# A filter network inside the preceding output projection, and a layer norm by token halves, in a four-layer encoder

## The reference

```python
for i in range(DEPTH):                       # 4 layers
    mod = silu(c) @ mod_w[i] + mod_b[i]
    shift, scale, gate = split(mod, 3)
    hn = rmsnorm(x, norm_g[i]) * (1 + scale) + shift
    # mixer i % 3: 0 = RWKV-7, 1 = Hyena, 2 = Conformer convolution
    x = x + gate * mixer(hn)                 # each mixer ends in (...) @ w_out
# Hyena filters: z from positions, three times z = sin(freq * (z @ W + b)), then (z @ f_w_out) * window, normalised, rfft
# Conformer:
a, b, g = split(h @ w_in, 3)
u = depthwise_conv(a * sigmoid(b), dw_w, dw_b)      # 31 taps
u = silu(layernorm(u, ln_g, ln_b))
return (u * silu(g)) @ w_out
```

## Time and profile before

| | |
|---|---|
| median of 3 runs | 4082.78 us (4078.05 to 4083.08) |
| the profiled execution | 4076.46 us, its span 4074.7 us |
| PE busy | 3435.6 us, 84% of the span |
| DVE busy | 2096.6 us, 51% |
| ACT busy | 1126.1 us, 28% |
| mean granted TensorE clock | 0.925 of full |

### The profile page before, as it was taken

One profiled execution on the slowest core, in us unless ns is written; L12 is line 12 of the kernel. 1 busy time (PEld: TensorE's weight loads), 2 busy tenths in 40 slices (PEclk: granted clock), 3 DMA queues, 4 the chain that ended last, 5 costly groups with the idle time before them and its releaser, 6 DMA issues. The chain is left out here.

```text
span 4074.7 us, 97171 instructions
## 1 busy us (share of the span) xinstructions
PE 3435.6 (84%) x41792; PEld 2461.1 (60%) x41792; DVE 2096.6 (51%) x4027; ACT 1126.1 (28%) x2792; POOL 0.2 (0%) x4
## 2 busy tenths in 40 slices
PE   4978888888888777989987899487788998889978
PEld 3556766766776644666664555254477667676665
DVE  2254544544454325776773299723455545555542
ACT  2023333332333222333231111112133333333330
POOL 0000000000000000000000000000000000000000
PEclk9988999999999888999998899688899999999989
DMA  3021101111111130010101111021000000000003
GB/s 142 31 80 50 66 26 46 60 33 45 55 50 40 62 108 29 30 43 32 33 36 52 64 52 52 16 89 41 27 14 19 19 12 14 14 19 18 13 20 106
DMA packets 65826, 179.05 MB, mean 44 GB/s; under 512 B 9105, under 2 KB 22545, under 8 KB 65425
## 3 DMA queue, kind: packets, MB, share of 16 engines
q1 hardware_dynamic: 53472, 144.02, 10.5%
q10 hardware_dynamic: 11952, 29.04, 1.9%
HBM read 157.30 MB, written 15.73 MB: 42 GB/s over the span
## 5 line engine op out<-in xcount | busy, mean ns | idle before, releaser
L1632 DVE SCALAR_TENSOR_TENSOR RBF<-bank,ID 128x256 bf16<-128x256 f32 x480 | 192.8, 421 | 409.6 <-PE bank L615 400.7
L954 PE MATMUL bank<-BY,W 128*128 128x384 f32 x1024 | 345.9, 498 | 48.0 <-DVEq L1709 35.2
L813 PE MATMUL bank<-BH,W 128*128 128x384 f32 x1024 | 342.8, 490 | 6.9 <-ACT HZ L1218 6.6
L954 PEld LDWEIGHTS bank<-BY,W 128*128 128x128 f32 x1024 | 196.7, 194 | 181.8 <-DVEq L1709 35.9
L813 PEld LDWEIGHTS bank<-BH,W 128*128 128x128 f32 x1024 | 191.8, 192 | 137.0 <-issue 16.7
L954 PE MATMUL bank<-BX,W 128*128 128x384 f32 x640 | 220.4, 500 | 61.4 <-DVE BX L1955 61.0
L1040 PE MATMUL bank<-BH,W 128*128 128x384 f32 x768 | 250.7, 490 | 15.8 <-DMA W<-in_cf_w_in 15.8
L1678 DVE SCALAR_TENSOR_TENSOR CACC<-CU,CV,CACC 128x798 f32<-128x798 f32 x232 | 224.1, 1041 | 0.0
L735 PE MATMUL bank<-BH,W 128*128 128x384 f32 x512 | 214.3, 549 | 8.9 <-DVE BH L1955 8.9
L1040 PEld LDWEIGHTS bank<-BH,W 128*128 128x128 f32 x768 | 147.2, 192 | 119.8 <-DMA W<-in_cf_w_in 16.9
L954 PEld LDWEIGHTS bank<-BX,W 128*128 128x128 f32 x640 | 121.3, 194 | 160.5 <-issue 67.6
(11 more groups left out here) (273 smaller groups left out, 6378.5 us busy)
## 6 DMA issues: line engine op xcount, KB each, us to landing
W<-in_mod_w SPq DMA_DIRECT2D x96, 512.0 KB, 3.6
W<-in_rw_w_in SPq DMA_DIRECT2D x68, 512.0 KB, 3.9
W<-in_hy_w_in SPq DMA_DIRECT2D x32, 512.0 KB, 6.8
x_scratch<-BX ACTq DMA_DIRECT2D x32, 384.0 KB, 4.2
W<-in_cf_w_in SPq DMA_DIRECT2D x24, 512.0 KB, 3.5
W<-in_rw_w_out SPq DMA_DIRECT2D x16, 512.0 KB, 4.2
W<-in_hy_w_out SPq DMA_DIRECT2D x8, 512.0 KB, 3.8
W<-in_cf_w_out SPq DMA_DIRECT2D x8, 512.0 KB, 4.2
```

Of the source, the lines that this page charges most:

```text
L813: mm = pe.matmul(pj(h), W[:, s, k, :], BH[:, k, tok(h)], start=(k == 0), stop=(k == KT - 1))
L954: mm = pe.matmul(pj(h), lhs(k), rhs(k, h), start=(k == 0), stop=(k == nk - 1))
L1632: v.scalar_tensor_tensor(RBF[:, d, :, :], xout(d), -1.0, bc(ID2[:, 1 if r < NBF else 0, :], GC), ALU.mult, ALU.add).then_inc(ir_ready, 1)
```

## The change

- The filter network of the Hyena layer runs inside the output projection of layer 0: its three matmul steps (`pe_mlp`) after products 0, 3 and 5, DVE's part in two pieces after each of tiles 1 to 6 (`dve_mlp`), ACT's sines after tiles 2, 4 and 6. It writes banks 4 and 5 in place of 2 and 3. DVE clears HU after tile 0. Its constants are loaded by SP between the first and second four weight tiles of that projection; the other Hyena constants, the first filter weights and the four weight tiles are issued behind the projection's, with no wait for BH. The two-tile buffer for x in layers 0 and 3 moves from TW to a part of HX.
- The vectors and first weight tiles of the Conformer are issued once the Hyena layer's outputs are complete, with no wait for BH.
- The layer norm of the Conformer: the mean is accumulated tile by tile inside the product loop (`means`, two tiles behind, banks 6 and 7). After it each step runs by token halves; the subtraction in four pieces. The squares are the loaded operand and one column of MEAN the moving one, so that the variance comes out token by token (3 columns per half); root and reciprocal are taken there, spread on a diagonal and multiplied out by PE, as in the RMS norm. Scale and root are applied in one instruction, and bias goes into the join and into ACT's tanh; the factor 0.25 goes into the gate vector.

```diff
-        XOUT = (TW, HZ, CACC)
+        XOUT = (HX[:, :, 0, :], HZ, CACC)
...
+        def before_hyena(l):
+            return l % 3 == 0 and l + 1 in layers
...
-        HY_CONST = ((ID, "idm"), (FWD, "hfwd"), (INV, "hinv"), (HZ[:, 0, :], "hz"), (HWF, "hwf"), (HB, "hb"), (HTW, "htw"), (HVA, "hyv"))
+        HY_MLP = ((HZ[:, 0, :], "hz"), (HWF, "hwf"), (HB, "hb"))
+        HY_CONST = ((ID, "idm"), (FWD, "hfwd"), (INV, "hinv"), (HTW, "htw"), (HVA, "hyv"))
...
-                    if first and s == 0:
-                        sp.wait_ge(h_ready, 2 * KT * (NRM[l] + 1))
-                        for dst, src in HY_CONST:
-                            sp.dma_start(dst[:], a[src]).then_inc(hyc_ready, 16)
-                        filt(j)
...
+            for dst, src in HY_CONST:
+                sp.dma_start(dst[:], a[src]).then_inc(hyc_ready, 16)
+            filt(0)
             one(0, True)
...
                 for s in range(slots):
                     load(s, source(0, s), free[s])
+                if between:
+                    between()
...
-                    sp.wait_ge(h_ready, 2 * KT * (NRM[l] + 1))
+                    sp.wait_ge(y_ready, NRM[l] * KT)
                     sp.dma_start(CVA[:, :, :], a["cfv"]).then_inc(cfv_ready, 16)
                     cf(0, True)
...
+                def mlp_constants():
+                    sp.wait_ge(y_ready, (NRM[l] + 1) * KT)
+                    for dst, src in HY_MLP:
+                        sp.dma_start(dst[:], a[src]).then_inc(hym_ready, 16)
+                tiles((l, "out"), 2, lambda i, s: cols(wout, i * 4 + s), None, mlp_constants if before_hyena(l) else None)
...
+        def pe_mlp(pe, i):
+            if i:
+                pe.wait_ge(mlp_sin, i)
+            else:
+                pe.wait_ge(hym_ready, 16 * len(HY_MLP))
+            for b, (n0, nt, ln) in enumerate(NTL):
+                mm = pe.matmul(NB[b][:, 0:ln], HWF[:, i, :], HZ[:, i % 2, n0 * P:n0 * P + ln], start=True, stop=True)
+            mm.then_inc(mlp_full, 1)
...
+                    if not chain:
+                        pe.wait_ge(mlp_sin, 3)
+                        pe.wait_ge(xn_ready, 2 * KT * (NRM[l] + 1))
...
-            for i in range(3):
-                if i:
-                    pe.wait_ge(mlp_sin, i)
-                else:
-                    pe.wait_ge(mlp_arg, 1)
-                for b, (n0, nt, ln) in enumerate(NTL):
-                    mm = pe.matmul(SC[b][:, 0:ln], HWF[:, i, :], HZ[:, i % 2, n0 * P:n0 * P + ln], start=True, stop=True)
-                mm.then_inc(mlp_full, 1)
-            pe.wait_ge(mlp_sin, 3)
...
+                    def means(k):
+                        pe.wait_ge(cf_conv, k + 1)
+                        for h in range(2):
+                            mm = pe.matmul((SQB, YB)[h][:, 0:HALF], MEAN, BD[:, k, tok(h)], start=(k == 0), stop=(k == KT - 1))
+                            if k == KT - 1:
+                                mm.then_inc(ln_mean, 1)
...
                                 mm.then_inc(cb_full[s][h], 1)
-                    base = plan[(l, "ln")][1]
-                    pe.wait_ge(cf_conv, KT)
-                    product(base, lambda k: MEAN, lambda k, h: BD[:, k, tok(h)], KT).then_inc(pj_full[1], 1)
+                            if s == 0 and j >= 2:
+                                means(j - 2)
+                    means(KT - 2)
+                    means(KT - 1)
                     for h in range(2):
-                        pe.wait_ge(pj_free[h], base + 2)
-                    for k in range(KT):
-                        pe.wait_ge(ln_sq, k + 1)
-                        for h in range(2):
-                            mm = pe.matmul(pj(h), MEAN, SQ[:, k % 2, tok(h)], start=(k == 0), stop=(k == KT - 1))
-                        mm.then_inc(ln_r, 1)
-                    pe.wait_ge(ln_r, KT)
-                    pe.sem_inc(pj_full[0], 1)
-                    pe.sem_inc(pj_full[1], 1)
+                        for k in range(KT):
+                            pe.wait_ge(ln_sq, h * KT + k + 1)
+                            for c in range(3):
+                                t = h * HALF + c * P
+                                mm = pe.matmul(SC[h][:, c:c + 1], SQ[:, k % 2, t:t + P], MEAN[:, 0:1], start=(k == 0 and c == 0),
+                                               stop=(k == KT - 1 and c == 2))
+                            mm.then_inc(ln_r, 1)
+                    for h in range(2):
+                        pe.wait_ge(ln_dg, h + 1)
+                        pe.matmul((SQB, YB)[h][:, 0:HALF], MEAN, SQ[:, 0, tok(h)], start=True, stop=True).then_inc(ln_full, 1)
...
+                        if before_hyena(l) and i * 4 + s in (0, 3, 5):
+                            pe_mlp(pe, (0, 3, 5).index(i * 4 + s))
...
-            act.activation(RN[:, 0, 0:1], EPSV[:, 0:1], ACT.Sqrt)
+            if not before_hyena(l):
+                act.activation(RN[:, 0, 0:1], EPSV[:, 0:1], ACT.Sqrt)
...
+                if before_hyena(l) and j in (2, 4, 6):
+                    i = j // 2 - 1
+                    act.wait_ge(mlp_arg, i + 1)
+                    act.activation(HZ[:, (i + 1) % 2, :], HZ[:, (i + 1) % 2, :], ACT.Sin).then_inc(mlp_sin, 1)
+                    if i == 2:
+                        act.activation(RN[:, 0, 0:1], EPSV[:, 0:1], ACT.Sqrt)
...
-                    act.wait_ge(ln_c, 1)
-                    for k in range(KT):
-                        if k >= 2:
-                            act.wait_ge(ln_r, k - 1)
-                        act.activation(SQ[:, k % 2, :], BD[:, k, :], ACT.Square).then_inc(ln_sq, 1)
+                    act.activation(RN[:, 0, 0:1], EPSV[:, 2:3], ACT.Sqrt)
                     for h in range(2):
-                        act.wait_ge(pj_full[h], base + 2)
-                        act.activation(RS[:, tok(h)], pj(h), ACT.Sqrt, bias=EPSV[:, 2:3]).then_inc(pj_free[h], 1)
-                    for k in range(KT):
-                        act.wait_ge(ln_t, k + 1)
-                        act.activation(TT[:, k % 2, :], BD[:, k, :], ACT.Tanh, scale=0.5).then_inc(cf_tanh, 1)
+                        for k in range(KT):
+                            act.wait_ge(ln_c, h * 2 + k // 4 + 1)
+                            if k >= 2:
+                                act.wait_ge(ln_r, h * KT + k - 1)
+                            act.activation(SQ[:, k % 2, tok(h)], BD[:, k, tok(h)], ACT.Square).then_inc(ln_sq, 1)
+                        act.wait_ge(ln_r, (h + 1) * KT)
+                        act.activation(RN[:, h, :], SC[h][:, 0:3], ACT.Sqrt, bias=EPSV[:, 2:3]).then_inc(ln_rt, 1)
+                    for h in range(2):
+                        for k in range(KT):
+                            act.wait_ge(ln_t, h * KT + k + 1)
+                            if k >= 2:
+                                act.wait_ge(ln_j, h * KT + k - 1)
+                            act.activation(CACC[:, k % 2, tok(h)], BD[:, k, tok(h)], ACT.Tanh, scale=0.5, bias=CLB[:, k:k + 1]).then_inc(cf_tanh, 1)
...
+        def dve_mlp(v, C, i, part):
+            two_pi_hi = 6.28125
+            two_pi_lo = float(2 * np.pi - two_pi_hi)
+            magic = 12582912.0
+            z, r = HZ[:, (i + 1) % 2, :], RS[:, :]
+            if part == 0:
+                v.wait_ge(mlp_full, i + 1)
+                for b, (n0, nt, ln) in enumerate(NTL):
+                    t = C.mark(v.tensor_scalar(z[:, n0 * P:n0 * P + ln], NB[b][:, 0:ln], HB[:, i:i + 1], HB[:, 3 + i:4 + i], ALU.add, ALU.mult))
+                C.wait(t)
+                C.link(v.tensor_scalar(r, z, float(1 / (2 * np.pi)), magic, ALU.mult, ALU.add))
+                C.link(v.tensor_scalar(r, r, magic, None, ALU.subtract))
+            else:
+                C.link(v.scalar_tensor_tensor(z, r, -two_pi_hi, z, ALU.mult, ALU.add))
+                C.link(v.scalar_tensor_tensor(z, r, -two_pi_lo, z, ALU.mult, ALU.add))
+                C.link(v.tensor_scalar(z, z, 3.1415925, -3.1415925, ALU.min, ALU.max))
+                v.sem_inc(mlp_arg, 1)
...
+                if before_hyena(l):
+                    if j == 0:
+                        C.link(v.memset(HU[:, :, :], 0.0))
+                    elif j < 7:
+                        dve_mlp(v, C, (j - 1) // 2, (j - 1) % 2)
...
+            mb = (SQB, YB)
+            gate = MOD[:, l * 24 + 16:l * 24 + 24, :]
+            C.mark(v.tensor_scalar(CLB[:, :], CVA[:, :, CONV + 2:CONV + 3].squeeze(2), 0.5, None, ALU.mult))
+            C.link(v.tensor_scalar(gate, gate, 0.25, None, ALU.mult))
+            def joined(k, h):
+                v.wait_ge(cf_tanh, KT * 2 + h * KT + k + 1)
+                v.scalar_tensor_tensor(BY[:, k, tok(h)], CACC[:, k % 2, tok(h)], 1.0, BY[:, k, tok(h)], ALU.add, ALU.mult).then_inc(ln_j, 1)
+                if h:
+                    v.wait_ge(ln_j, KT + k + 1)
+                    v.sem_inc(y_ready, 1)
+            v.wait_ge(ln_mean, 2)
             for h in range(2):
-                v.wait_ge(pj_full[h], base + 1)
```

(62 more changed lines are left out.)

6 lines of the change are left out of this document (2 added, 4 removed).

## The result

The changed kernel takes 4040.5 us (median; 4037.3 to 4047.5), the kernel before in the same comparison 4082.9: ratio 0.9897, 95% interval 0.9878 to 0.9917. It is faster, by 42 us. The forecast was 4012, 71 us faster, and the time lies outside the range. The profiled execution took 4037.31, its span is 4035.5.

A forecast was written before the change was run, and what follows sets the result against it. PE, busy 84% of the span, was taken to bound the kernel; gains of 45.0 + 15.8 + 10.1 = 70.9 us off the 4082.78 median gave 4012, range 3995 to 4029.

The forecast's parts named there:

- The sum at the three places: Forecast gains at the start of the Hyena layer, start of the Conformer layer and layer norm: 45.0 + 15.8 + 10.1 us.
- rival B: Layer norm gives nothing: its final loop stalls between VectorE and ScalarE, 2.3 us per half tile, not 1.7; 4022, chance 0.12.
- the forecast's own bounds: Likeliest case with all three gains at their upper or lower bounds: 45.0 + 17.0 + 14.5 (4006), 40.3 + 13 + 5 (4024).
- Hyena start: First Hyena products start with BH, gaining 49.0 us; the filter network costs 4.0 in the output projection: 45.0 net.
- rival C: Output projection: filter network isn't hidden, layers two and three wait in PE's queue for their sine; 4025, chance 0.07.
- Conformer start: Weights fetched before the norm, so PE starts at the first BH, 2294.65 in place of 2310.49: gain 15.8 us.
- Rival D: Conformer layer's start: early weight fetch doesn't bring PE forward, something behind the landing was late too; 4028, chance 0.05.
- The wait for cf_conv: Conformer loop: new wait in PE's queue before `means` asks for the tile two back and is met, 19 us to spare.
- Rival E: Conformer loop: the wait for cf_conv ties PE to VectorE, costing 83 us over seven tiles; 4095, slower, chance 0.03.
- Layer norm: Last convolution tile to first output product: shorter mean, squares 20.6 us, final loop 27 us; gain 10.1, from 5 to 14.5.
- Rivals A: Layer norm: the unbroken string of squares brings the clock to 2.4 GHz, 8 us less; 4004, chance 0.15.

The follow-up runs named there:

- the last two runs: Changed kernel, both pair loops moved, 42 unread products added, final loop's second-half join counted on y_ready; first also with products among the squares: 3991.3 and 3988.5 us.

## Why the prediction was wrong

The sum at the three places was 70.9 us and is 68.1 (42.2 and 25.9 of the table). With it alone the time would have been near what the changed kernel takes with layer 3's loop moved: 4009.4, forecast 4012. (A slip in the range: rival B's 4022 lies inside the forecast's own bounds, 4006 to 4024, not outside.) Point by point:

- **Hyena start**, forecast 45.0: 43.7 up to the second product, 42.2 over the layer. The network costs 4.5 us in the projection (1.45 and twice 1.54, forecast 4.0), at the high clock and with no wait, so rival C is out. The first half of the first product runs fast (2.6 us better than priced), the filter products wait 0.8 us for the norm, and the gap for the bank is longer than I had it, 3.3 us in place of 1.9; the clock does fall in it, which I had left to the bounds. Where the 1.5 us between 43.7 and 42.2 go stays open.
- **Conformer start**, forecast 15.8: 16.7 by the kernel with that wait put back. Rival D is out.
- **The wait for cf_conv** holds nothing up: the mean of a tile takes 1.45 us inside the loop and the loop's pace is unchanged. Rival E is out.
- **Layer norm**, forecast 10.1: 8.9. Mean 2.93, squares 20.8: as priced. The final loop took 28.5 in place of 27; the self-wait in the second half, 1.8 us by the last two runs, covers the difference. Rivals A (squares fast) and B (nothing gained) are out.
- **The step that failed** is the sentence "Everything behind each place is a chain through PE or VectorE and moves up with it." It moved up by 67 us and then ran slower: 4.7 us per tile of layer 3's pair loop, 28 in all. I had counted what the added instructions cost where they run and not what they do by being there. VectorE's program grew by 18 slots ahead of a loop that had 8 to spare. No rival had this. The profile of before did show it: six waits of 3.2 us put down to "issue" at layer 0's back edges and none at layer 3's, in the same code, and two more in the Hyena loop; I had read none of these rows.

## What to carry to other kernels

Where a kernel has loops on an engine and a change adds or takes instructions ahead of them, look where the loops lie: count slots, and look for "issue" ahead of the first instruction of an iteration and for packets on the instruction queue q14 that come once per iteration. A stall of 3.2 us there costs more than itself if another engine hangs on it: here 4.7 us, since the clock of TensorE falls. Look at every loop that way, and don't stop at the ones that your rule names: the Hyena loop's two stalls stand in every trace here, and I took my rule for complete without them. And compare a change with the loops in the same place in both kernels, or its gain is mixed with that of a shift: the same edit was worth 42 us here, or some 70 with layer 3's loop free of stalls on both sides (66.5 by the spans of the two profiled executions, 74 by the medians), and 72 idle waits were worth more (31) than two of its three parts together.

## What the runs showed of the hardware that I had not expected

- A loop of 292 or 298 slots (18.2 or 18.6 KB) on VectorE stalls 3.1 to 3.5 us at every back edge or at none, by where it lies in the program; one of 344 slots stalled at both back edges in all of the three places where it lay. Each stall brings 5 packets of 8 KB on q14 (41, 71 and 100 packets for 0, 6 and 12 stalls of the pair loops). Four blocks of 128 slots stall and three don't, with borders 8 slots ahead of where the compiled program's own count puts them: that is worked out from which loops stalled, not read anywhere.
- TensorE's granted clock fell to 0.50 and stayed there for 20 us in which TensorE was busy for 19.87, with products of one column and a few of 128. The Trainium skill, in "TensorE: Matmul & The Clock Gate", section "Part 1: The HAM clock gate", says that activity releases the throttle; here busy time alone did not.
